# Branch projections over six blocks of 128 rows, the output gate packed to 128 columns, and the branches in the order first, third, second

## The chip, the cores and the metric

The kernel runs on one core of one Trainium2 chip. The metric is the device time of one launch in microseconds. Five engines work side by side: TensorE (PE, with its weight loads shown as PEld), VectorE (DVE), ScalarE (ACT), GpSimd (POOL) and SyncE (SP, which here only issues transfers).

## The reference

Two transformer-like blocks run one after the other on 256 tokens of width 1024. The change lies in the second block, between its input projection and its output projection:

```python
z = h @ w_in[l]                                   # sections: rnn, q, k, v, g, dec, mq, gate
z_rnn, z_q, z_k, z_v, z_g, z_dec, z_mq, z_gate = jnp.split(z, split_idx, axis=-1)
out_a = rg_lru(causal_dwconv(z_rnn, ...), ...)    # gated linear recurrence over the tokens
o_gla = rms_norm(chunked_gla(...), gla_norm[l].reshape(GLA_HEADS, GLA_DV)).reshape(bsz, slen, -1)
out_b = o_gla * jax.nn.silu(z_g)
out_c = ...                                       # attention over mem, 4 heads of 192
branches = jnp.stack([out_a, out_b, out_c], axis=2)            # each 768 wide
proj = jnp.einsum("bsnc,ncd->bsnd", branches, w_branch[l])     # 768 -> 1024, three times
gates = jax.nn.sigmoid(z_gate).reshape(bsz, slen, N_BRANCHES, D_MODEL)
merged = jnp.sum(gates * proj, axis=2)
x = x + merged @ w_out[l]
```

## The kernel before

Every dense product runs weight-stationary over the transposed activations: a weight tile of 128 output columns is [128 rows, 8 blocks, 128 columns] in float32. Each tile is split into a high and a low part in a reduced format (`w_hi`, `w_lo`), each activation likewise, and three products are added: high weights by high and low activations, low weights by high activations. So a tile costs PE 3 x 8 matmuls with 256 moving columns (L629 for the first 16, L634 for the last 8).

The weights pass through a chain of four engines. SP loads a tile into `raw` (L491; two chunks of two tiles each in flight), ACT rounds it into `w_hi` (`round_tile`, L1188, or L1183 and L1185 for a packed tile), POOL subtracts it from `raw` into `w_lo` (`subtract`, L448, or L443 and L444), and PE multiplies. A chunk is two tiles (v = 0, 1). There is one `w_hi` and one `w_lo` for each v: ACT may overwrite `w_hi[v]` when PE has finished its 16 high products, POOL may overwrite `w_lo[v]` when PE has finished the tile, and SP may reload `raw` when POOL has subtracted. The order on each engine is written out by hand: `look_ahead(n)` makes ACT round all tiles up to chunk n at that place of its program; the sections stand in the order of `plan_chunks`.

Widths of 768 are kept as eight blocks of 96 rows (`C96`, `K96 = 8`), so `out_a`, `out_b` and `out_c` fill 96 of 128 partitions and a branch tile is [96 rows, 8 blocks, 128 columns]. Sections in `PACKED` (the recurrence's input `z_rnn`, `zqk`, `zmq`, `mem_k`) spread their eight 96-column tiles over six tiles of 128 columns: the last two tiles are loaded apart into `spare` (L500) and appended as 32 columns each; `evacuate_packed` puts the 32 spilled rows back by two more copies (L1216). The output gate `zg` is not packed: it has eight tiles of 96 columns in four chunks.

What touches the change, in program order of the second block: `z_rnn`, `dec` (a 16-column product, L683), `zqk`, `zv`, `zmq` with the recurrence's gates between, `gate0` beside the memory attention, `zg` beside the linear attention's states (`gla_states`), then `gla_out` (L1061, L1069) and `branch0` in turn, `gate1`, `branch1`, `gate2`, `branch2`, `out2`. On DVE stand in this order: `recur` (the scan, L2163), `silu(0)` and `silu(1)` (L2181), `gla_states(0)` and `(1)` (L2189, L2195), the low part of `out_a` (`rest_parts`, L1739), `silu(2)`, `gla_states(2)` (L2195), `silu(3)`; then the four merges of `branch0` (L2215), the norm of `out_b` (L2233, L2238), its product with the gate (L2242), the low parts of `out_b` and `out_c` (L1739), and the merges (L2217, L2221) with the low parts of `merged` (L2226). ACT rounds the high parts of `out_a`, `out_b` and `out_c` (`round_parts`, L1168) and of `merged` (L1618), and evacuates the gates from PSUM (L1205). PE waits for `outb_split` before `branch1`, for `m_rounded` inside the first product of `out2` (L650).

## Time and profile before

| | us |
|---|---|
| median of 3 runs | 1716.06 (1712.99 to 1716.21) |
| the profiled execution | 1715.97 |
| its span in the trace | 1714.0 |
| PE busy | 1663.0 (97%) |
| DVE / ACT / POOL busy | 1035.4 / 895.0 / 905.3 |

The span is what lies between the first and the last instruction of the trace; 2 us of the run lie outside it. "Busy" of PE is a share of time with a matmul in flight. The stage that the change touches goes from about 1176 to 1468 us of the span.

### The profile page before, as it was taken

How to read it: one execution, taken by the hardware profiler on the slowest of the kernel's cores; microseconds unless marked ns; L12 is line 12 of the kernel's file. 1: busy time of each engine (PE TensorE's matmuls, PEld its weight loads, DVE VectorE, ACT ScalarE, POOL GpSimd, SP SyncE). 2: the span in 40 equal slices, each digit the busy share in tenths (PEclk: the TensorE clock that was granted, in tenths of full speed). 3: DMA queues.
4: the chain of work that ended last, by engine and by line, in shares of the span. 5: the costliest groups of instructions: out<-in, count | busy, mean ns of one | idle time of the engine just before them, and what ended most of it. 6: DMA issues, size and time to landing. Idle time of an engine off the chain costs nothing.

```text
span 1714.0 us, 33864 instructions
## 1 busy us (share of the span) xinstructions
PE 1663.0 (97%) x12837; PEld 1556.6 (91%) x12837; DVE 1035.4 (60%) x1801; ACT 895.0 (52%) x1218; POOL 905.3 (53%) x411
## 2 busy tenths in 40 slices
PE   8998899999999999999999999999999999899997
PEld 7997899899999999998888888898989999799997
DVE  5996755239921777778888666657455263534321
ACT  4555765455555444444444445465676544466652
POOL 7785358668887000000000344467855688588885
PEclk9999999999999999999999999999999999999999
DMA  5564235455556555545555666654533445455663
GB/s 180 169 187 138 75 120 172 146 168 183 183 183 183 169 164 171 161 157 173 174 176 174 209 190 190 192 187 129 161 108 102 124 141 155 135 172 184 183 185 111
DMA packets 80696, 277.02 MB, mean 162 GB/s; under 512 B 10320, under 2 KB 12640, under 8 KB 80608
## 3 DMA queue, kind: packets, MB, share of 16 engines
q1 hardware_dynamic: 80336, 274.76, 51.5%
q8 instruction: 59, 0.97, 0.2%
q0 software_dynamic: 272, 1.05, 0.2%
q14 instruction: 29, 0.24, 0.0%
HBM read 274.73 MB, written 1.05 MB: 161 GB/s over the span
## 4 chain that ended last, share of the span: by engine, by line
PE 88%; DVE 5%; POOL 3%; issue 2%; ACT 1%; DMA 0%; SPq 0%; DVEq 0%; POOLq 0%; ACTq 0%
PE gemm L629 35%; PE gemm L878 20%; PE gemm L634 17%; PE aux L1126 4%; PE gemm L697 3%; PE aux L854 2%; POOL w_lo L448 2%; POOL w_lo L443 1%; PE gemm L661 1%; PE aux L715 1%; DVE big L1724 0%; PE gemm L650 0%; POOL w_lo L444 0%; DVE big L1838 0%; PE aux L823 0%
## 5 line engine op out<-in xcount | busy, mean ns | idle before, releaser
L448 POOL TENSOR_TENSOR w_lo<-raw,w_hi 128x1024 fp32r<-128x1024 f32 (+2 forms) x340 | 825.7, 2435 | 378.8 <-ACT w_hi L1188 367.4
L1188 ACT ACTIVATE w_hi<-raw 128x1024 fp32r<-128x1024 f32 (+2 forms) x500 | 526.5, 1056 | 633.0 <-PE gemm L629 322.5
L629 PE MATMUL gemm<-h_hi,w_hi 128*128 128x256 f32 (+1 forms) x2256 | 325.5, 287 | 1.5 <-PE aux L823 0.7
L629 PE MATMUL gemm<-h_lo,w_hi 128*128 128x256 f32 (+1 forms) x2304 | 324.5, 284 | 0.4 <-DVE mem_lo L1739 0.4
L634 PE MATMUL gemm<-h_hi,w_lo 128*128 128x256 f32 (+1 forms) x2256 | 317.6, 283 | 3.4 <-POOL w_lo L444 2.4
L629 PEld LDWEIGHTS gemm<-h_lo,w_hi 128*128 128x128 f32 (+1 forms) x2304 | 297.9, 192 | 1.0 <-DVE mem_lo L1739 0.9
L629 PEld LDWEIGHTS gemm<-h_hi,w_hi 128*128 128x128 f32 (+1 forms) x2256 | 292.9, 192 | 4.7 <-issue 2.9
L634 PEld LDWEIGHTS gemm<-h_hi,w_lo 128*128 128x128 f32 (+1 forms) x2256 | 290.5, 191 | 5.0 <-POOL w_lo L444 2.8
L448 DVE TENSOR_TENSOR w_lo<-raw,w_hi 128x1024 fp32r<-128x1024 f32 x160 | 195.3, 1222 | 115.5 <-ACT w_hi L1188 113.0
L878 PE MATMUL gemm<-w_hi,h_hi 128*128 128x512 f32 x1024 | 256.7, 393 | 0.0
L878 PEld LDWEIGHTS gemm<-w_hi,h_hi 128*128 128x128 f32 x1024 | 189.8, 188 | 38.1
L580 POOL DMA_DIRECT2D small<-in_memT x1 | 1.0, 1029 | 397.6 <-DVE big L1999 397.6
L878 PE MATMUL gemm<-w_lo,h_hi 128*128 128x512 f32 x512 | 136.9, 389 | 0.0
L2005 DVE TENSOR_TENSOR h_hi<-big,h_hi 128x512 fp32r<-128x512 f32 x64 | 89.3, 1395 | 51.2 <-ACT h_hi L1378 51.2
L878 PEld LDWEIGHTS gemm<-w_lo,h_hi 128*128 128x128 f32 x512 | 96.1, 188 | 20.2
L1769 DVE SCALAR_TENSOR_TENSOR aux<-big,params,aux 128x256 f32<-128x256 f32 x240 | 94.4, 481 | 0.0
L2270 DVE SCALAR_TENSOR_TENSOR big<-gemm,params,big 128x255 f32<-128x255 f32 (+1 forms) x96 | 39.7, 476 | 80.8 <-ACT big L1633 80.8
L443 POOL TENSOR_TENSOR w_lo<-raw,w_hi 128x768 fp32r<-128x768 f32 x24 | 47.1, 1962 | 17.1 <-ACT w_hi L1185 16.9
L1991 DVE TENSOR_TENSOR small<-small 128x512 f16<-128x512 f16 x128 | 50.5, 436 | 0.0
L1988 DVE TENSOR_TENSOR small<-small 128x1024 f16<-128x1024 f16 x64 | 43.8, 685 | 0.0
L1999 DVE SCALAR_TENSOR_TENSOR big<-aux,big 128x512 f32 x64 | 43.8, 684 | 0.0
L854 PEld LDWEIGHTS aux<-small 128*128 128x128 f16 x1024 | 34.5, 97 | 9.7 <-issue 8.1
(359 smaller groups left out, 2010.8 us busy)
## 6 DMA issues: line engine op xcount, KB each, us to landing
raw<-in_w_u SPq DMA_DIRECT2D x128, 512.0 KB, 3.5
raw<-in_w_ev SPq DMA_DIRECT2D x128, 512.0 KB, 3.7
raw<-in_w_up SPq DMA_DIRECT2D x48, 512.0 KB, 4.3
raw<-in_w_gate SPq DMA_DIRECT2D x24, 512.0 KB, 3.6
raw<-in_w_down SPq DMA_DIRECT2D x24, 512.0 KB, 4.3
raw<-in_w_branch SPq DMA_DIRECT2D x24, 384.0 KB, 3.3
raw<-in_w_conv_in SPq DMA_DIRECT2D x16, 512.0 KB, 4.1
raw<-in_w_peer_q SPq DMA_DIRECT2D x16, 512.0 KB, 4.2
```

What stands on the lines that cost most here:

```text
L443: eng.tensor_tensor(lo[:, :, 0:C96], by_k(raw[c.raw][v], C96), hi[:, :, 0:C96], ALU.subtract)
L448: eng.tensor_tensor(w_lo[v][0:rows, 0:n], raw[c.raw][v][0:rows, 0:n], w_hi[v][0:rows, 0:n], ALU.subtract).then_inc(lo_ready[v], 1)
L629: mm = pe.matmul(out, w[:, k, :], act_part[:, k, :], start=(n == k == 0), stop=False)
L634: mm = pe.matmul(out, w[:, k, :], x[0][:, k, :], start=False, stop=(k == KD - 1))
L697: mm = pe.matmul(pair(gemm[c.bank])[:, tt, :], x[:, v * KD // 2 + k, tt * P:(tt + 1) * P], w[:, k, :], start=(begins and tt == k == 0), st ...
L854: mm = pe.matmul(aux[b][:, n * P // 2:(n + 1) * P // 2], hot2[:, b, n // 2, :, n % 2], hot1[:, b, part, n // 2, :, n % 2], start=(part == ...
L878: mm = pe.matmul(gemm[2 * half + tt][:, :], a[:, c.raw, v, tt * P:(tt + 1) * P], w[v][:, half * (D // 2):(half + 1) * (D // 2)], start=Fal ...
L1126: mm = pe.matmul(pair(aux[pr])[:, v, :], w[v][:, k * P:(k + 1) * P], x[:, g * KD + k, :], start=(g == v == k == 0 and w is w_hi and x is f ...
L1188: act.activation(w_hi[v][0:rows, 0:n], raw[c.raw][v][0:rows, 0:n], ACT.Copy).then_inc(hi_ready[v], 1)
L1769: ins = dve.scalar_tensor_tensor(acc, zc[:, k, w:w + T], tap, acc, ALU.mult, ALU.add)
L1991: ins = dve.tensor_tensor(hot1[:, b, part], hot, along(gate_parts[:, part, tokens], P // 2), ALU.mult)
L2005: dve.tensor_tensor(a_lo[:, c.raw, :, :], act_peer[:, plane, :], a_hi[:, c.raw, :, :], ALU.subtract).then_inc(a_split, 1)
```

## The change

It has four parts.

1. **Branch products.** `out_a`, `out_b` and `out_c` get 128 partitions. The last two of their eight blocks of 96 rows are folded into partitions 96 to 127 of the first six, so each is [128 rows, 6 blocks]. A branch weight tile becomes [128 rows, 6 blocks, 128 columns], loaded in three transfers (96 rows of 3 KB, and twice 32 rows of three pieces of 512 bytes). PE does 3 x 6 matmuls for a tile where it did 3 x 8. For `out_a` ACT does the fold by three copies, for `out_c` it is in the last copy from PSUM (three for one), for `out_b` DVE's norm does it (12 instructions for 8).
2. **Output gate.** `zg` is packed: three chunks of 128-column tiles for four of 96. ACT and POOL handle a tile in two instructions; `sg` holds [128, 6, 256] and matches the folded `out_b`. POOL's mask of the scores goes ahead of the third chunk, and DVE does `gla_states(2)` ahead of `silu(2)`.
3. **Order.** The sections run `gate2`, `branch2`, `gate1`, `branch1`; the parts of `out_c` are made before the norm of `out_b`, and the last merges are those of `branch1`.
4. **One rounding moved.** ACT rounds the two tiles of `zqk`'s first chunk before it evacuates the third chunk of `z_rnn`.

```diff
-    for name, count in (("zqk", 3), ("zv", 3), ("zmq", 3), ("gate0", 4), ("zg", 4), ("branch0", 4),
-                        ("gate1", 4), ("branch1", 4), ("gate2", 4), ("branch2", 4), ("out2", 4)):
-        section(name, count)
+    for name, count in (("zqk", 3), ("zv", 3), ("zmq", 3), ("gate0", 4), ("zg", 3), ("branch0", 4),
+                        ("gate2", 4), ("branch2", 4), ("gate1", 4), ("branch1", 4), ("out2", 4)):
+        section(name, count, transfers=3 if name.startswith("branch") else 1)
...
-        a_parts = (x_hi[0:C96], f_hi[0:C96, third[0], :])
+        KB = MW // P
+        a_parts = (x_hi[:, 0:KB, :], f_hi[:, third[0], :][:, 0:KB, :])
...
-        PACKED = ("mem_k", "z_rnn", "zqk", "zmq")
+        PACKED = ("mem_k", "z_rnn", "zqk", "zmq", "zg")
...
+        def fold(tile, j):
+
+            return tile[C96:P, j:KB:KB // 2, :], slice(j * FOLD, (j + 1) * FOLD)
...
+                if c.index in folded:
+                    tile = raw[c.raw][v]
+                    sp.dma_start(tile[0:C96, 0:KB * P], src[:, 0:KB * P]).then_inc(landed[c.raw][v], 16)
+                    for b in range(2):
+                        half = KB // 2 * P
+                        dst = tile[C96:P, b * half:(b + 1) * half].rearrange("r (j m) -> r j m", m=P)
+                        src_b = src[:, (KB + b) * P:(KB + b + 1) * P].rearrange("(j r) m -> r j m", r=FOLD)
+                        sp.dma_start(dst, src_b).then_inc(landed[c.raw][v], 16)
+                    return
...
-                for k in range(KD):
-                    mm = pe.matmul(out, w[:, k, :], x[0][:, k, :], start=False, stop=(k == KD - 1))
+                w = by_k(w_lo[v], m, n=steps)
+                for k in range(steps):
+                    mm = pe.matmul(out, w[:, k, :], x[0][:, k, :], start=False, stop=(k == steps - 1))
...
             for i, c in enumerate(plan["z_rnn"]):
+                look_ahead(plan["zqk"][0].index if i == 2 else c.index + 1)
                 evacuate_packed(c, zr[:, 2 * i:2 * i + 2, RNN_CONV - 1:], zr[:, 6:8, RNN_CONV - 1:])
...
                     act.wait_ge(rnn_done, 1)
-                    round_parts(a_parts[0], out_a, outa_rounded)
+                    for j in range(KB // 2):
+                        dst, rows = fold(all_a, j)
+                        act.activation(dst, out_a[rows, KB:K96, :], ACT.Copy).then_inc(a_folded, 1)
+                    act.wait_ge(a_folded, KB // 2)
+                    round_parts(a_parts[0], all_a, outa_rounded, tiles=KB)
...
-            for i in range(4):
-                if i == 3:
-                    act.wait_ge(out_b_done, 1)
-                    round_parts(b_parts[0], out_b, outb_rounded)
-                gate_evac(1, i)
             act.wait_ge(mo_moved, MH)
-            round_parts(c_parts[0], out_c, outc_rounded)
-            look_ahead(plan["gate2"][0].index)
+            round_parts(c_parts[0], all_c, outc_rounded, tiles=KB)
             for i in range(4):
                 gate_evac(2, i)
-
             for i in range(4):
-                look_ahead(plan["branch2"][i].index + 1)
+                if i == 1:
+                    act.wait_ge(out_b_done, 1)
+                    round_parts(b_parts[0], all_b, outb_rounded, tiles=KB)
+                gate_evac(1, i)
...
-            rest_parts(a_parts[1], out_a, a_parts[0], outa_rounded, outa_split)
+            rest_parts(a_parts[1], all_a, a_parts[0], outa_rounded, outa_split, tiles=KB)
+            gla_states(2)
             silu(2)
-            gla_states(2)
-            silu(3)
```

How the instructions of ACT stand between `z_rnn` and `dec` (L1213 and L1216 take a chunk out of PSUM, L1183 and L1185 round a packed tile, L1205 takes out `dec`). Before, from the evacuation of the second chunk of `z_rnn` on:

```order
L1213 ACTIVATE big<-gemm 96x2x256
L1216 ACTIVATE big<-gemm 32x256 x2
L1213 ACTIVATE big<-gemm 96x2x256
L1216 ACTIVATE big<-gemm 32x256 x2
L1183 ACTIVATE w_hi<-raw 128x8x96
L1185 ACTIVATE w_hi<-big 128x8x32
L1183 ACTIVATE w_hi<-raw 128x8x96
L1185 ACTIVATE w_hi<-big 128x8x32
L1205 ACTIVATE big<-gemm 16x256
```

Of the same place in the changed kernel (its line numbers are 20 higher):

```order
L1233 ACTIVATE big<-gemm 96x2x256
L1236 ACTIVATE big<-gemm 32x256 x2
L1203 ACTIVATE w_hi<-raw 128x8x96
L1205 ACTIVATE w_hi<-big 128x8x32
L1203 ACTIVATE w_hi<-raw 128x8x96
L1205 ACTIVATE w_hi<-big 128x8x32
L1233 ACTIVATE big<-gemm 96x2x256
L1236 ACTIVATE big<-gemm 32x256 x2
L1225 ACTIVATE big<-gemm 16x256
```

The four roundings moved ahead of the second evacuation. On DVE, from the scan to the merges of `branch0`, before:

```order
L2181 TENSOR_TENSOR big<-big,gemm 96x512 x2
L2189 COPY big<-aux 96x2x192 x2
L2195 SCALAR_TENSOR_TENSOR big<-big,aux 96x192 x4
L1739 TENSOR_TENSOR f_hi<-big,x_hi 96x1024 x2
L2181 TENSOR_TENSOR big<-big,gemm 96x512
L2195 SCALAR_TENSOR_TENSOR big<-big,aux 96x192 x4
L2181 TENSOR_TENSOR big<-big,gemm 96x512
L2215 TENSOR_TENSOR big<-big,gemm 128x512 x4
```

and in the changed kernel:

```order
L2211 TENSOR_TENSOR big<-big,gemm 128x512 x2
L2219 COPY big<-aux 96x2x192 x2
L2225 SCALAR_TENSOR_TENSOR big<-big,aux 96x192 x4
L1769 TENSOR_TENSOR f_hi<-big,x_hi 128x768 x2
L2225 SCALAR_TENSOR_TENSOR big<-big,aux 96x192 x4
L2211 TENSOR_TENSOR big<-big,gemm 128x512
L2244 TENSOR_TENSOR big<-big,gemm 128x512 x4
```

One of the gate products is gone and the last states stand ahead of the one that is left. On DVE again, from the merges of `branch0` to the first later merge, before:

```order
L2215 TENSOR_TENSOR big<-big,gemm 128x512 x4
L2233 RECIPROCAL big<-big 96x1024
L2238 SCALAR_TENSOR_TENSOR big<-big,params 96x256 x8
L2242 TENSOR_TENSOR big<-big 96x2048
L1739 TENSOR_TENSOR f_hi<-big,x_lo 96x1024 x2
L1739 TENSOR_TENSOR f_lo<-big,f_hi 96x1024 x2
L2217 TENSOR_TENSOR big<-big,gemm 128x512
```

and in the changed kernel:

```order
L2244 TENSOR_TENSOR big<-big,gemm 128x512 x4
L1769 TENSOR_TENSOR f_lo<-big,f_hi 128x768 x2
L2263 RECIPROCAL big<-big 96x1024
L2268 SCALAR_TENSOR_TENSOR big<-big,params 96x256 x6
L2274 SCALAR_TENSOR_TENSOR big<-big,params 32x256 x6
L2278 TENSOR_TENSOR big<-big 128x1536
L2246 TENSOR_TENSOR big<-big,gemm 128x512
```

The low parts of `out_c` (`f_lo`) moved ahead of the norm; those of `out_b` (`f_hi` from `x_lo`) moved behind the four merges of `branch2`.

## Rows read from the trace of the kernel before

**Rows 1.** The page: the span, and the chain that ended last by engine.

```profile
span 1714.0 us, 33864 instructions
PE 88%; DVE 5%; POOL 3%; issue 2%; ACT 1%; DMA 0%; SPq 0%; DVEq 0%; POOLq 0%; ACTq 0%
```

**Rows 2.** Windows: width, busy PE, PEld, DVE, ACT, POOL (x), granted clock, DMA, GB/s.

```profile
1193.00:1198.00 5.00, 2.98 (x22) 2.39 (x20) 5.00 (x9) 1.25 (x4) 5.00 (x3) 1.00 0.25 84
1198.00:1202.00 4.00, 4.00 (x23) 4.00 (x23) 4.00 (x3) 0.80 (x2) 4.00 (x3) 0.58 0.51 139
1385.00:1398.00 13.00, 9.71 (x75) 9.10 (x76) 9.67 (x6) 8.53 (x10) 10.79 (x4) 1.00 0.23 63
1464.00:1468.00 4.00, 4.00 (x23) 4.00 (x24) 0.49 (x1) 2.33 (x3) 0.40 (x1) 0.61 0.10 39
```

**Rows 3.** The chain in time order, one gate tile: start, length, engine, count.

```profile
1412.08 1.91 PE gemm L629 x16
1413.99 0.96 PE gemm L634 x8
```

**Rows 4.** Timeline, end of `gate1`, start of `branch1`: start, length, instruction, [idle before <-releaser].

```profile
1362.45 6.54 DVE L2233 RECIPROCAL big<-big 96x1024 f32<-96x1024 f32 x1
...
1369.03 10.71 DVE L2238 SCALAR_TENSOR_TENSOR big<-big,params 96x256 f32<-96x256 f32 x8
...
1379.77 4.38 DVE L2242 TENSOR_TENSOR big<-big 96x2048 f32<-96x2048 f32 x1
...
1385.27 2.35 DVE L1739 TENSOR_TENSOR f_hi<-big,x_lo 96x1024 fp32r<-96x1024 f32 x2 [1.13 <-ACT x_lo L1168]
...
1387.68 1.21 PE L629 MATMUL gemm<-x_lo,w_hi 96*128 96x256 f32 x8 [2.85 <-DVE f_hi L1739]
```

**Rows 5.** Timeline around the first tile of `zqk`.

```profile
1185.31 3.68 SPq L491 DMA_DIRECT2D raw<-in_w_zq  x3
...
1191.34 0.85 ACT L1183 ACTIVATE w_hi<-raw 128x768 fp32r<-128x768 f32 x1
...
1194.39 3.15 POOL L444 TENSOR_TENSOR w_lo<-big,w_hi 128x256 fp32r<-128x256 f32 x1
...
1197.59 1.27 PE L634 MATMUL gemm<-h_hi,w_lo 128*128 128x256 f32 x8 [2.02 <-POOL w_lo L444]
```

**Rows 6.** Timeline from the recurrence's scan to the first instruction of `gla_out`.

```profile
1309.57 7.94 DVE L2163 TENSOR_TENSOR_SCAN big<-big 96x256 f32<-96x256 f32 x8
...
1321.04 5.01 DVE L1739 TENSOR_TENSOR f_hi<-big,x_hi 96x1024 fp32r<-96x1024 f32 x2
...
1326.57 1.38 DVE L2195 SCALAR_TENSOR_TENSOR big<-big,aux 96x192 f32<-96x192 f32 x4
...
1328.09 1.57 PE L1061 MATMUL aux<-small,big 64*96 64x64 f32 x32
```

**Rows 7.** Groups by shape, 1130 to 1320 us: count, busy, mean ns, idle before.

```profile
L448 POOL TENSOR_TENSOR w_lo<-raw,w_hi 128x768 fp32r<-128x768 f32 x6 | 11.5, 1929 | 11.0 <-ACT w_hi L1188 10.4 <-PE gemm L634 0.6
...
L1216 ACT ACTIVATE big<-gemm 32x256 f32<-32x256 f32 x24 | 9.1, 378 | 0.3
L1185 ACT ACTIVATE w_hi<-big 128x256 fp32r<-128x256 f32 x22 | 8.8, 402 | 0.0
```

**Rows 8.** DMA issues of the whole run: count, KB each, median us to landing.

```profile
raw<-in_w_branch SPq DMA_DIRECT2D x24, 384.0 KB, 3.3
...
big<-in_rg_w_a SPq DMA_DIRECT2D x1, 288.0 KB, 3.2
...
big<-in_gla_w_decay SPq DMA_DIRECT2D x1, 24.0 KB, 3.9
```

**Rows 9.** Timeline, end of `branch2` and start of `out2`.

```profile
1445.66 15.57 POOL L448 TENSOR_TENSOR w_lo<-raw,w_hi 96x1024 fp32r<-96x1024 f32 x6 [2.25 <-ACT w_hi L1188]
...
1454.18 7.60 DVE L2226 TENSOR_TENSOR m_lo<-big,x_hi 128x512 fp32r<-128x512 f32 x1
...
1463.82 0.51 PE L650 MATMUL gemm<-x_hi,w_hi 128*128 128x256 f32 x2 [2.75 <-ACT x_hi L1618]
```

More of the change, by code:

```diff
@@ L463, in spare_columns @@
             return spare[:, n // 3, :, n % 3 * SPILL:(n % 3 + 1) * SPILL]
-        floats = {c.index: NARROW.get(name, TILE) for name, chunks in plan.items() for c in chunks}
-        tile_rows = {c.index: C96 for name in ("branch0", "branch1", "branch2") for c in plan[name]}
+        floats = {c.index: TILE for c in order}
+        FOLD = P - C96
+        folded = {c.index for name in ("branch0", "branch1", "branch2") for c in plan[name]}
+        floats.update({n: KB * P for n in folded})
+        def fold(tile, j):
+            return tile[C96:P, j:KB:KB // 2, :], slice(j * FOLD, (j + 1) * FOLD)
         ITS = P // (2 * BANKS)
@@ L1090, in _ @@
                     pe.wait_ge(outa_split, 2)
-                    product(plan["branch0"][h0 + i], P, x=a_parts, rows=C96)
+                    product(plan["branch0"][h0 + i], P, x=a_parts, steps=KB)
+            for c in plan["gate2"]:
+                product(c, P)
+            pe.wait_ge(outc_split, 2)
+            for c in plan["branch2"]:
+                product(c, P, x=c_parts, steps=KB)
             for c in plan["gate1"]:
```

119 lines of the change are left out of this document (66 added, 53 removed).

## The prediction

> **What bounds the kernel now.** I read the chain that ended last first: 88% of it is PE [rows 1]. So a matmul taken out of a stretch where PE never waits is worth its own length, and where PE waits, the wait ends when the engine ahead of it ends. The chain in order of time gives the length: 16 matmuls in 1.91 us and 8 in 0.96 us, 0.12 us each, 2.87 us a tile [rows 3]. Then I looked for the places in the touched stage where PE does less than one matmul in 0.12 us. There are four. (1) At 1193 to 1198 us it does 22, and the low products of the first tile of `zqk` wait 2.02 us for POOL [rows 2, 5]; in the 4 us after that the granted clock is 0.58, so PE spends most of them at the lower of its two levels (1.2 for 2.4 GHz), and 23 matmuls are done where 33 would fit [rows 2]. (2) Around 1328 us PE hardly waits, but DVE's chain from the scan ends at 1327.95 and PE's `gla_out` starts at 1328.09 [rows 6]: PE and DVE arrive together, so work taken from PE alone ahead of that point gains nothing. (3) Between 1385 and 1398 us 75 matmuls are done where 109 would fit [rows 2]; PE waits 2.85 us for the low part of `out_b` [rows 4]. (4) At the start of `out2` PE waits 2.75 us for the last part of `merged` [rows 9], and the 4 us after it have a granted clock of 0.61 [rows 2].
>
> **The branch products.** There are 3 sections of 4 chunks of 2 tiles, 24 tiles, and each loses 6 of 24 matmuls: 144 x 0.12 = 17.3 us. A tile then takes PE 18 x 0.12 = 2.15 us. It counts in full only if the three engines behind the weights keep up.
> POOL subtracts [128, 768] in 1929 ns on average [rows 7], under 2.15, where it took 2.60 us a tile in the last branch section (six in 15.57 us [rows 9]). The bounds of what POOL costs are nothing and 24 x (2.60 - 2.15) = 10.8 us; the near row is the one of the same width, so I take 1.0 us, for the last section, where ACT waits for DVE's merge before it rounds on.
> ACT's rounding shrinks with the width (0.85 us for 768 columns [rows 5]) and is well covered.
> The load is the new risk: three transfers for one, on SP's one queue. A buffer's cycle is landing, rounding 0.85, subtraction 1.93 and some 0.4 of handing over, 3.2 us plus the landing, in which PE does four tiles: it binds above 4 x 2.15 - 3.2 = 5.4 us of landing. The whole tile lands in 3.3 us now. The nearest row for short pieces is the load of the recurrence's gate weights, 768 pieces of 384 bytes in 3.2 us, and the third transfer issued right behind it and its twin landed in 3.9 us [rows 8]. With two more issues ahead (under 0.4 us each in the queue) I get 3.9 + 0.7 = 4.6 us: not binding, cost nothing. If it binds, the price is a rival's.
> The Trainium skill speaks against this edit: "DMA: Bandwidth & Descriptors", section Bandwidth, advises large transfers and calls those under 64 KB dominated by their descriptors; two of the three are 48 KB. By the fit in its section on the anatomy of a DMA (about 2.0 us and bytes over 436e3), three in a row would take an estimated 2.7 + 2.1 + 2.1 = 6.9 us, a tile (6.9 + 3.2) / 4 = 2.5 us, and the time would be about 1699 us. The trace's three loads in a row overlap, which speaks for the sum above.
> The fold itself: for `out_c` three copies for one on ACT (378 ns for 256 columns [rows 7], some 0.6 for 512), beside PE's next tiles, nothing. For `out_b` see the order.
>
> **The output gate.** Eight tiles become six: 48 matmuls, 5.8 us of PE. But place (2) says that DVE's chain sets the end. It starts when ACT has rounded the second chunk of `zg` and made the root, now one instruction of 402 ns [rows 7] longer: the scan ends at about 1317.9. ACT then folds `out_a` in three copies (1.8 us) and rounds it in two of 768 columns (1.7): 1321.4, which is when DVE comes free of its states (1321.04 and the 0.4 later [rows 6]). So the fold hides behind DVE, just. The low part of `out_a` took 5.01 us against POOL and 2.35 without it for 1024 columns a piece [rows 4, 6]; three quarters of these are 3.8 and 1.8, for the folded width. The states take 1.38. `gla_out` starts between 1324.6 and 1326.6 in place of 1328.09: a gain of 1.5 to 3.5 us, **2.4**. PE's own work ends before that even with the wait for the first states that shorter cover opens. The bounds are 3.5, and below nothing, -1, if ACT's longer row of copies comes after DVE. What is late next is DVE still.
>
> **The order.** Now `out_b` is ready 21.7 us after the last merge of `branch0`: 6.54 + 10.71 + 4.38 [rows 4]; `gate1` covers 23 us, so its rounding and low part stick out. Afterwards DVE first makes the low parts of `out_c` (2 to 4 us), then 6.54, then twelve instructions at 1.34 = 16.1, then three quarters of 4.38 = 3.3: some 30 us. `branch1` comes 23.0 + 17.2 + 23.0 = 63 us after. The wait goes: 34 missing matmuls, **4.0 us**. `branch2` needs `out_c`, done 5 us into the 23 of `gate2`. DVE's long row now ends 30 us after, when the first merge of `branch2` could go at 27.3; behind it wait four merges, and their PSUM banks are wanted again only at 40, so that costs nothing; without this cover it would be 3 us. On ACT the wait for `out_b` stands behind the first evacuation of `gate1`, at 43 us: over by then. The two roundings of `out_c` put ACT back 1.7 us in a stretch where it has more than that to spare.
>
> **The rounding moved.** ACT rounds the first tile of `zqk` at 1191.34, behind the evacuation of `z_rnn`; its load was issued at 1185.31 [rows 5], so it should be there by 1189 or so. POOL then starts up to 2.4 us earlier, and the 2.02 us wait goes. If the load lands only at 1191, nothing is gained. The pause goes with it, and I expect the clock to stay: 10 matmuls more in the 4 us, 1.2 us. Together **3.2 us**, bounds 0 and 3.5. The evacuations move back by up to 3 us; the convolution on DVE waits for them, but it ends long before its next reader.
>
> **The tail** (4) I leave as it is. DVE's `m_lo` took 7.60 us while POOL ran six subtractions without a pause [rows 9]; a free pair took 2.35 for twice the width each [rows 4]. The Trainium skill ("SBUF — State Buffer", SBUF: two separate sides) has VectorE with two SBUF inputs and GpSimd take one port pair for a whole instruction each, and the trace agrees. What shorter subtractions change here is a rival.
>
> **The sum** against the profiled execution, 1715.97 us (its span 1714.0; the median is 1716.06, so the two agree): -17.3 + 1.0 - 2.4 - 4.0 - 3.2 = -25.9, so **1690 us**.
>
> **Rivals.** *The tail frees itself*: POOL's shorter instructions let `m_lo` in, the last merge is on time, PE's 2.75 us and the 1.2 us at the low clock go: 1686. For it: a gap of 0.2 us in each 2.15. Against: POOL is as busy as before, relative to PE. *POOL binds*: with DVE against it a subtraction keeps 2.6 us, 10.8 for 1.0: 1700. For it: rows 9. Against: rows 7. *The loads line up* so that each waits for the one ahead: 3.3 + 3.9 + 3.9 = 11.1 us of landing, (11.1 + 3.2) / 4 = 3.6 us a tile against 2.87 before, 24 x 0.73 = +17.5, with the other gains of 9.6: 1724, **slower**. It decides from a landing of 8.3 us (branches gain nothing) and 9.9 (the whole is slower). Against: the three loads in a row of rows 8. *The short loads wait for the long one* and overlap each other only: 3.3 + 3.9 = 7.2 us of landing, (7.2 + 3.2) / 4 = 2.6 us a tile, 24 x 0.45 = 10.8 of the 17.3 given back: 1701. This is where the page's rule on small transfers would lead, by its own figures to 1699. *It does not do what it says*: `zg` and the rounding bring nothing (DVE's chain and the load set those ends): 1690 + 2.4 + 3.2 = 1696.
>
> **Chances.** The forecast 0.60, the tail 0.10, POOL 0.11, no gain outside the branches 0.10, short loads behind the long one 0.05, the loads in a row 0.04. The range 1683 to 1700 takes in the first four but for their edges, 0.85 in all. A difference of 0.2% (3.4 us) is about what a measurement of this kernel can tell from none: faster 0.95, same 0.01, slower 0.04.
>
> **What would show it.** A branch tile of 18 matmuls in 2.15 us with no wait of PE for POOL or ACT longer than 0.5 us; landing of the branch loads under 5.4 us; no wait at `branch1`, none of 2 us at `zqk`, the clock 1.0 after it; `gla_out` 2 us earlier relative to the scan. It is wrong if PE waits inside the branch sections, or if ACT comes late with `out_a`.

## The result, and the profile after

| | median of the runs shown | lowest to highest | profiled execution | its span |
|---|---|---|---|---|
| before | 1714.53 us (4) | 1712.80 to 1716.21 | 1715.97 us | 1714.0 us |
| after | 1683.37 us (4) | 1683.01 to 1686.05 | 1683.40 us | 1681.7 us |

The ratio is 0.9822 (95% interval 0.9805 to 0.9839): 1.8% faster, well over the 0.2% that a measurement can tell. The prediction said 1690 us, 25.9 us under the profiled execution of before; the profiled executions are 32.6 us apart. So the direction and the range hold, and 6.7 us more went than the sum has terms for. The rest of this document finds them.

Page of the kernel after: the span, and the chain that ended last, by engine.

```profile
span 1681.7 us, 33548 instructions
PE 90%; DVE 5%; POOL 2%; issue 2%; ACT 1%; DMA 0%; SPq 0%; DVEq 0%; ACTq 0%; POOLq 0%
```

PE is still the bound, and more of it than before [rows 1]. The windows that answer to [rows 2], with the same columns: the first two at `zqk`, the last two at the start of `out2`.

```profile
1191.00:1196.00 5.00, 5.00 (x41) 4.73 (x40) 5.00 (x6) 2.79 (x6) 4.20 (x3) 1.00 0.68 203
1196.00:1200.00 4.00, 4.00 (x35) 4.00 (x35) 4.00 (x4) 3.09 (x6) 3.85 (x4) 1.00 0.44 139
...
1428.00:1432.00 4.00, 2.68 (x20) 2.50 (x21) 3.94 (x3) 1.94 (x3) 4.00 (x2) 1.00 0.73 193
1432.00:1436.00 4.00, 3.90 (x30) 3.49 (x29) 1.71 (x2) 2.12 (x4) 1.07 (x2) 1.00 0.69 209
```

PE does one matmul in some 0.12 us at `zqk`, and the granted clock is 1.00 in all four, where before it was 0.58 and 0.61 after the two waits. To find where the time went I take the start of the same instruction in both traces and follow how the distance between them grows:

| place (start of) | before | after | distance | grown by | forecast |
|---|---|---|---|---|---|
| product of `dec`, ahead of the touched stage | 1189.83 | 1187.72 | 2.11 | 2.11 | 0 |
| decay's matmuls, behind `zqk` | 1214.62 | 1208.74 | 5.88 | 3.77 | 3.2 |
| first `gla_out` | 1328.09 | 1318.54 | 9.55 | 3.67 | 2.4 |
| first product of `out2` | 1458.35 | 1428.54 | 29.81 | 20.26 | 17.3 + 4.0 - 1.0 = 20.3 |
| second chunk of `out2` | 1469.00 | 1436.00 | 33.00 | 3.19 | 0 |
| a product of `up` | 1501.28 | 1469.04 | 32.24 | -0.76 | 0 |

The branches and their order came out as the sum has them. Four things need an explanation: 2.1 us ahead of every touched line, the size of the `zqk` and `zg` terms, and the 3.2 us at `out2`, which the forecast left as it was and one rival gave away.

### The profile page after: what moved, and what is told of

Same layout as the page of the kernel before. It is cut to its first block, busy times and chain, and to the rows that moved or that the text cites. A ratio compares the mean times of both kernels' runs of the same rounds, so it can differ in the third digit from the quotient of the medians.

```text
span 1681.7 us, 33548 instructions
## 1 busy us (share of the span) xinstructions
PE 1638.4 (97%) x12645; PEld 1532.3 (91%) x12645; DVE 1043.7 (62%) x1804; ACT 892.5 (53%) x1226; POOL 894.2 (53%) x415
## 4 chain that ended last, share of the span: by engine, by line
PE 90%; DVE 5%; POOL 2%; issue 2%; ACT 1%; DMA 0%; SPq 0%; DVEq 0%; ACTq 0%; POOLq 0%
PE gemm L649 35%; PE gemm L898 21%; PE gemm L654 18%; PE aux L1146 4%; PE gemm L717 3%; PE aux L874 2%; POOL w_lo L451 1%; PE gemm L681 1%; PE aux L735 1%; DVE big L1754 0%; PE aux L843 0%; PE gemm L703 0%; PE gemm L670 0%; DVE big L1868 0%; DVE big L2193 0%
## 5 line engine op out<-in xcount | busy, mean ns | idle before, releaser
L451 POOL TENSOR_TENSOR w_lo<-raw,w_hi 128x1024 fp32r<-128x1024 f32 (+1 forms) x332 | 800.6, 2420 | 350.9 <-ACT w_hi L1208 339.2
L1208 ACT ACTIVATE w_hi<-raw 128x1024 fp32r<-128x1024 f32 (+1 forms) x492 | 515.6, 1050 | 619.4 <-PE gemm L649 308.0
L649 PE MATMUL gemm<-h_hi,w_hi 128*128 128x256 f32 x2240 | 322.8, 287 | 1.6 <-PE aux L843 0.7
L649 PE MATMUL gemm<-h_lo,w_hi 128*128 128x256 f32 x2288 | 322.6, 284 | 0.4 <-DVE mem_lo L1769 0.4
L654 PE MATMUL gemm<-h_hi,w_lo 128*128 128x256 f32 x2240 | 315.5, 283 | 1.4 <-POOL w_lo L451 0.9
L649 PEld LDWEIGHTS gemm<-h_lo,w_hi 128*128 128x128 f32 x2288 | 296.4, 193 | 1.0 <-DVE mem_lo L1769 0.9
L649 PEld LDWEIGHTS gemm<-h_hi,w_hi 128*128 128x128 f32 x2240 | 290.6, 192 | 4.8 <-issue 3.0
L654 PEld LDWEIGHTS gemm<-h_hi,w_lo 128*128 128x128 f32 x2240 | 288.9, 192 | 3.1 <-POOL w_lo L451 1.8
L447 POOL TENSOR_TENSOR w_lo<-raw,w_hi 128x768 fp32r<-128x768 f32 x30 | 58.8, 1961 | 19.9 <-ACT w_hi L1205 18.5
```

The costliest lines, as they stand in the source:

```text
L447: eng.tensor_tensor(lo[:, :, 0:C96], by_k(raw[c.raw][v], C96), hi[:, :, 0:C96], ALU.subtract)
L451: eng.tensor_tensor(w_lo[v][:, 0:n], raw[c.raw][v][:, 0:n], w_hi[v][:, 0:n], ALU.subtract).then_inc(lo_ready[v], 1)
L649: mm = pe.matmul(out, w[:, k, :], act_part[:, k, :], start=(n == k == 0), stop=False)
L654: mm = pe.matmul(out, w[:, k, :], x[0][:, k, :], start=False, stop=(k == steps - 1))
L1208: act.activation(w_hi[v][:, 0:n], raw[c.raw][v][:, 0:n], ACT.Copy).then_inc(hi_ready[v], 1)
```

## The 2.1 us that the change did not make

The distance is there at 170 us already, in the attention of the first half, on the same instructions (2.40 us; 0.39 of it at 154 us). DVE splits a row of 16 x 256 numbers into parts there while POOL subtracts. The third cast in the trace of before, and in that of after:

```profile
163.21 4.73 POOL L448 TENSOR_TENSOR w_lo<-raw,w_hi 128x1024 fp32r<-128x1024 f32 x2 [1.60 <-ACT w_hi L1188]
...
163.23 2.51 DVE L1798 CAST big<-big 16x256 bf16<-16x256 f32 x1
```

```profile
162.86 0.28 DVE L1828 CAST big<-big 16x256 bf16<-16x256 f32 x1
...
163.16 4.71 POOL L451 TENSOR_TENSOR w_lo<-raw,w_hi 128x1024 fp32r<-128x1024 f32 x2 [1.91 <-ACT w_hi L1208]
...
163.18 2.44 DVE L1831 COPY big<-big 16x256 bf16<-16x256 bf16 x1
```

POOL's two subtractions started at 163.21 in the trace of before and at 163.16 in that of after. The same cast takes 0.28 us when it starts just ahead of POOL's subtraction and 2.5 us when it starts just behind it, since it then waits for the whole of it; so does the copy behind it in either case. A few tenths of a microsecond decide over some 2. The Trainium skill ("SBUF — State Buffer", SBUF: two separate sides) has the pair of ports that VectorE and GpSimd share taken for a whole instruction by whoever starts first; the trace agrees. Whether chance did this, and not the change, I tested with the changed kernel itself.

### The changed kernel again

> The changed kernel itself again, as the yardstick for the two runs beside it. 1683.3 us where the small copies of the attention stage fall the short way and 1685.5 to 1686 where they fall the long way; the runs should show both.

1684.86 us median (1683.50 to 1685.94, 5 runs), beside 1716.11 of before. Its profiled execution took 1685.94 us. Timeline of it:

```profile
163.69 2.50 DVE L1828 CAST big<-big 16x256 bf16<-16x256 f32 x1
...
168.72 1.38 PE L776 MATMUL aux<-big 128*128 128x128 f32 x4 [3.50 <-DVE big L1831]
```

The same program, the other outcome, 2.5 us more, and PE waits 3.5 us for these copies in place of 1.1. So before was profiled with the long outcome and after with the short one. The outcome is the larger part of what differs ahead of the touched stage, but not all of it: from 154 us to 170 it makes 2.0 us between the two traces of the changed kernel, another 0.8 is there ahead of it, and what moves that was not looked for. To set only the long executions side by side is therefore not enough, since `changed_again` came to the product of `dec` 0.98 us later than before did. What holds is the distance from that product on. The table has it for the traces of the experiments that follow, each against the kernel that it was made from: where the product starts, and how much later than in that kernel (minus: earlier) the trace is further on, with the distance at the product taken off.

| trace | against | outcome | product of `dec` | decay's matmuls | first `gla_out` | first of `out2` | second chunk of `out2` |
|---|---|---|---|---|---|---|---|
| `changed_again` | after (1187.72) | long | 1190.81 | 0.0 | 0.0 | 0.0 | 0.0 |
| `round_back` | after | short | 1188.35 | 2.3 | 2.3 | 2.6 | 2.5 |
| `silu_back` | after | short | 1188.04 | 0.0 | 2.3 | 6.7 | 6.6 |
| `old_order` | after | long | 1188.03 | 0.0 | 0.0 | 5.4 | 5.3 |
| `rows_96` | after | long | 1189.60 | 0.0 | 0.0 | 0.2 | 0.2 |
| `one_transfer` | after | long | 1188.63 | 0.0 | 0.0 | 0.3 | 0.3 |
| `loads_held` | after | long | 1190.78 | 0.0 | 0.0 | 8.1 | 7.7 |
| `order_only` | before (1189.83) | short | 1187.46 | 0.0 | 0.0 | -4.1 | -5.6 |
| `columns_768` | before | long | 1190.33 | 0.0 | 0.0 | -0.1 | -3.6 |
| `rows_128` | before | long | 1190.34 | 0.0 | 0.0 | 1.9 | -1.5 |

By this measure the change is worth 30.1 us with the trace of after (32.24 less 2.11) and 30.7 with that of `changed_again`, both at the product of `up`; the sum missed 4.2 to 4.8 us of it, not 6.7. The 0.6 between the two is the clock behind the norm: 0.87 from 1457 to 1469 in the one, 1.00 from 1460 to 1472 in the other.

### POOL held back at that place

```diff
+                    if c is plan["ga"][2]:
+                        subtract(pool, c, tiles=(0,))
+                        pool.wait_ge(c_ready, 1)
+                        subtract(pool, c, tiles=(1,))
+                        continue
```

The first attempt had the wait one chunk too early, at `ga[1]`:

> The changed kernel in which POOL, between the two subtractions of the second chunk of ga, waits until DVE has made the parts of the forget gate's sums. Mine: three small DVE instructions took 2.4 us each there since each waited for a whole subtraction; with POOL held back only the first does, the parts are ready 4.3 us earlier, PE's waits of 1.1 and 4.9 us in that stage shrink by about 4, the time is 1683.3 - 4 = 1679, and all runs lie within 1 us, because no instruction starts beside a subtraction by chance. Rival: POOL's later subtraction makes PE wait instead, and the time stays at 1683; or the small instructions are slow by themselves, and nothing changes but the wait.

1687.39 us (1685.17 to 1688.48). All small instructions took 0.22 to 0.41 us, with POOL silent, which settles that they are not slow by themselves; but that chunk's subtraction was wanted earlier, and PE paid for it:

```profile
154.88 0.28 DVE L1833 CAST big<-big 16x256 bf16<-16x256 f32 x1
...
159.64 2.07 PE L659 MATMUL gemm<-h_hi,w_lo 128*128 128x256 f32 x8 [5.55 <-POOL w_lo L451]
```

The second:

> As pool_waits, but one chunk later: there the wait stood in front of a subtraction that PE needed before the forget gate's sums were ready (PE waited 5.6 us for it), while the subtractions that DVE's small instructions ran into are those of the third chunk of ga. POOL now waits between the two tiles of that chunk. Mine: the first small instruction waits 2.4 us for the first subtraction, all later ones take 0.2 to 0.4, the parts are ready 4.3 us earlier, POOL's second subtraction starts at about 161.3 and ends at 163.7, when PE wants it, and the time is 3 to 4 us under the changed kernel's shorter level, 1679.5. The runs lie closer together than the changed kernel's. Rival: DVE's row of 8 multiplications behind it collides with POOL's subtractions instead, and less than 1 us is left of the gain.

1684.42 us (1682.44 to 1685.07) beside 1684.86 of the changed kernel on the same chip: no difference, where 1679.5 was expected. The parts were ready 4 us earlier, but the eight multiplications behind them now met POOL's subtractions. First the row with POOL held back, then that of the kernel after:

```profile
163.16 7.99 DVE L1845 SCALAR_TENSOR_TENSOR big<-big,params,rstd 128x256 f32<-128x256 f32 x8
```

```profile
167.44 3.48 DVE L1840 SCALAR_TENSOR_TENSOR big<-big,params,rstd 128x256 f32<-128x256 f32 x8
```

The rival of that expectation came true: the collision was moved, not removed. As long as POOL has as many subtractions to make in that stretch, someone on DVE waits for them here.

## The experiments on the four parts

### The rounding of zqk's first tile, put back

```diff
             for i, c in enumerate(plan["z_rnn"]):
-                look_ahead(plan["zqk"][0].index if i == 2 else c.index + 1)
                 evacuate_packed(c, zr[:, 2 * i:2 * i + 2, RNN_CONV - 1:], zr[:, 6:8, RNN_CONV - 1:])
```

> The changed kernel with the rounding of zqk's first tile put back behind the evacuations of z_rnn. Mine: the place gained 3.8 us by the two traces (2.0 us of waiting, the rest clock), so 1683.3 + 3.8 = 1687.1 us, PE waits about 2 us for POOL at zqk and the 4 us after that have a granted clock near 0.6. Rival (the place is only earlier because everything ahead of it is): under 1 us, 1684, no wait. A second thing to read here: in the attention stage of the first half DVE's small copies start either just before or just after a subtraction of POOL, which by the two traces is worth 2.2 us; the profile should show either 0.28 or 2.5 us for the second cast, and its time should lie on the 1687 or the 1689 side accordingly.

1687.16 us median (1686.07 to 1689.53). The profiled one took 1686.73 with the short outcome, 3.3 over 1683.40. Timeline of it, and under it the window behind the wait:

```profile
1196.14 1.22 PE L654 MATMUL gemm<-h_hi,w_lo 128*128 128x256 f32 x8 [2.05 <-POOL w_lo L448]
```

```profile
1196.50:1200.50 4.00, 4.00 (x36) 4.00 (x35) 4.00 (x3) 1.99 (x5) 4.00 (x3) 1.00 0.53 123
```

The wait is back, as long as in [rows 5], but the clock after it is 1.00 here and was 0.58 in [rows 2]. By positions the place costs 2.3 us (2.94 behind `zqk`, 0.63 of them there ahead of it). So the edit is worth 2.3 us, its wait, and 1.5 more in an execution where the clock also falls. In the four traces of kernels with the old rounding in the kernel before (it, `order_only`, `columns_768`, `rows_128`) the stretch from the product of `dec` to the decay's matmuls took 24.8 us, in this one 23.3 and in the changed kernel 21.0. So all four had the 1.5; why this execution was spared is not shown.

Of the kernel after, the load and the rounding of that tile:

```profile
1183.22 3.68 SPq L508 DMA_DIRECT2D raw<-in_w_zq  x3
...
1186.39 0.85 ACT L1203 ACTIVATE w_hi<-raw 128x768 fp32r<-128x768 f32 x1 [2.68 <-DMA raw<-in_w_zq]
```

ACT waits for the load and rounds it 3.2 us after its issue; before, 6.0 us [rows 5]. That the tile would be there in time was the open point of this term.

### The output gate: DVE's row ahead of gla_out

Timeline of the kernel after, from the scan to `gla_out`; it answers to [rows 6].

```profile
1305.28 6.47 DVE L2193 TENSOR_TENSOR_SCAN big<-big 96x256 f32<-96x256 f32 x6
...
1315.28 1.82 DVE L1769 TENSOR_TENSOR f_hi<-big,x_hi 128x768 fp32r<-128x768 f32 x2
1317.01 1.38 DVE L2225 SCALAR_TENSOR_TENSOR big<-big,aux 96x192 f32<-96x192 f32 x4
1318.72 0.69 DVE L2211 TENSOR_TENSOR big<-big,gemm 128x512 f32<-128x512 f32 x1 [0.33 <-ACT big L1594]
```

The low part starts 3.5 us after the scan's end, as before, so the fold did hide. It takes 1.82 us where it took 5.01: mostly ahead of POOL this time. And the multiplication of the third gate pair, 0.69, now stands behind the states; before it lay between the low part and them. The prediction's sum goes from the low part straight to the states, so it took that 0.6 us out of the row without saying so, and did not ask what else the exchange of the two lines does. Putting it back:

```diff
-            gla_states(2)
             silu(2)
+            gla_states(2)
```

> The changed kernel with the multiplication of the third gate pair put back ahead of the last states on DVE. Mine: it costs its own 0.6 us in the row that gla_out waits for and nothing else, so gla_out starts 7.4 us after the end of the scan in place of 6.8, and the time is 0.6 us more, 1684.9, which the times alone can't tell from the changed kernel's 1684.3. Rival: it falls into the time that DVE waits for ACT anyway, gla_out at 6.8.

1690.11 us median (1689.41 to 1692.32), profiled 1690.32 with the short outcome: 6.9 us over the changed kernel (0.3 of it there ahead of the touched stage), where 0.6 was expected. Timeline of it, and under it the windows from `gla_out` on:

```profile
1319.03 0.69 DVE L2211 TENSOR_TENSOR big<-big,gemm 128x512 f32<-128x512 f32 x1 [1.61 <-ACT big L1594]
...
1321.16 2.83 PE L1081 MATMUL aux<-small,big 64*96 64x64 f32 x32 [2.80 <-DVE big L2225]
```

```profile
1320.00:1324.00 4.00, 2.84 (x33) 2.75 (x33) 1.01 (x4) 0.80 (x1) 0.88 (x1) 0.55 0.73 197
1324.00:1328.00 4.00, 4.00 (x25) 4.00 (x26) 0.00 (x0) 1.94 (x6) 0.00 (x0) 0.50 0.00 0
1328.00:1332.00 4.00, 4.00 (x26) 4.00 (x26) 0.00 (x0) 1.50 (x3) 0.31 (x1) 0.67 0.00 0
```

The multiplication needs ACT's third sigmoid, and this now ends late, behind the three folds, two roundings and a rounding of weights. DVE waits 1.61 us for it, the states stand behind that wait, PE waits 2.80 in place of 0.49, and its clock then falls to the lower of its two levels for most of 12 us. `gla_out` starts 2.3 us later by it; between there and `out2` another 4.3 is lost, in a stretch in which PE has no further wait over 0.5 us. So the fold on ACT, "hidden, just" in the sum, is hidden only because this line was moved with it. With it in its old place the gain of the packed gate (3.67) would have become a loss, by these two traces.

### The order of the branches

Old order in the changed kernel (the plan, PE's loops, ACT's and DVE's rows around them; the core of it):

```diff
-                        ("gate2", 4), ("branch2", 4), ("gate1", 4), ("branch1", 4), ("out2", 4)):
+                        ("gate1", 4), ("branch1", 4), ("gate2", 4), ("branch2", 4), ("out2", 4)):
...
-            for i in range(4):
-                merge(2, i)
             rest_parts(b_parts[1], all_b, b_parts[0], outb_rounded, outb_split, tiles=KB)
+            rest_parts(c_parts[1], all_c, c_parts[0], outc_rounded, outc_split, tiles=KB)
             for i in range(4):
                 merge(1, i)
+            for i in range(4):
+                merge(2, i)
```

> The changed kernel with the branches in the order first, second, third again and the low part of out_c behind that of out_b. Mine: the wait for out_b comes back, 4 us less what the shorter low part gives, 1683.3 + 3.5 = 1687, with a stretch ahead of branch1 in which PE waits 2 to 3 us for DVE, and a low clock after it. On the tail: theory A (shorter subtractions let m_lo in) keeps m_lo under 3 us each and no wait of 2 us at out2. Theory B (the order does it) brings the wait of 2.75 us at out2 back and the time to about 1690.

1688.80 us median (1688.05 to 1690.92), 3.9 over the 1684.86 of the changed kernel (on another chip, where before takes 1715.91 for 1716.11); profiled 1688.80 with the long outcome, 2.9 over 1685.94. But this execution came to the touched stage 2.8 us earlier than that one; from there on it loses 5.3 us (the table above). Timeline of it, and PE's windows around the wait's end and behind it:

```profile
1373.65 0.97 PE L649 MATMUL gemm<-x_lo,w_hi 128*128 128x256 f32 x6 [3.82 <-DVE f_hi L1770]
```

```profile
1372.00:1376.00 4.00, 2.35 (x15) 2.32 (x16) 2.41 (x3) 4.00 (x7) 2.72 (x2) 0.85 0.01 2
1376.00:1380.00 4.00, 4.00 (x27) 4.00 (x27) 2.87 (x3) 1.47 (x2) 4.00 (x2) 0.72 0.65 177
```

The wait for `out_b` comes back, and the clock behind it falls. In the kernel after there is none; the last row of DVE's long row, and PE's first product of `branch1`:

```profile
1378.28 3.42 DVE L2278 TENSOR_TENSOR big<-big 128x1536 f32<-128x1536 f32 x1
...
1409.76 0.87 PE L649 MATMUL gemm<-x_lo,w_hi 128*128 128x256 f32 x6
```

The row ends at 1381.7. The last merge of `branch0` ran at 1346.48, so it took 35 us where the prediction had 30 (twelve instructions against POOL took 18.0 us and not 16.1, and the low part of `out_c` 5.9 and not 2 to 4), and it is over 28 us before `branch1`.

The new order alone, in the kernel before (the same lines the other way round):

> The kernel before with the new order of the branches alone, subtractions and products as long as before. Mine: the wait for out_b goes, 1716 - 4.0 = 1712 (or 1713 - 4.0 = 1709 where the attention stage falls the short way). On the tail: theory A (shorter subtractions) leaves one m_lo of 5 to 8 us and a wait of PE of 2 to 3 us at out2. Theory B (the order) frees it, and the time is a further 3 us lower, 1709 or 1706.

1710.49 us median (1708.11 to 1711.36) beside 1715.91, ratio 0.9971 (0.9961 to 0.9982): 5.4 us by the medians, 4.0 forecast. By positions 4.1 us are gained up to `out2`, and 1.5 more behind its start. The low part and the wait there are as they were before, but the clock behind the wait is not: 1.00, where [rows 2] has 0.61.

```profile
1447.71 7.58 DVE L2225 TENSOR_TENSOR m_lo<-big,x_hi 128x512 fp32r<-128x512 f32 x1
...
1457.33 0.51 PE L650 MATMUL gemm<-x_hi,w_hi 128*128 128x256 f32 x2 [2.74 <-ACT x_hi L1617]
```

```profile
1457.00:1461.00 4.00, 3.67 (x30) 3.67 (x31) 0.91 (x2) 3.41 (x5) 0.51 (x1) 1.00 0.18 68
```

### The tail

Timeline of the kernel after at the end of `branch1` and the start of `out2`; it answers to [rows 9].

```profile
1418.33 14.22 POOL L451 TENSOR_TENSOR w_lo<-raw,w_hi 128x768 fp32r<-128x768 f32 x6 [2.03 <-ACT w_hi L1208]
...
1425.17 2.34 DVE L2255 TENSOR_TENSOR m_lo<-big,x_hi 128x512 fp32r<-128x512 f32 x1
...
1428.54 0.47 PE L670 MATMUL gemm<-x_hi,w_hi 128*128 128x256 f32 x2 [0.56 <-ACT w_hi L1208]
```

POOL works without a pause here too (six in 14.22 us, the last two on 1024 columns), and yet `m_lo` waits for one of them only, not for three. (The row of six in [rows 9] holds two of the 128 x 1024 tiles of `out2` as well, its last two, from 1456.5 on. They are the ones that went ahead of the waiting `m_lo`, at the end of the last subtraction on 96 x 1024.) `old_order` showed the same (its `m_lo` at most 2.89 us, no wait for `x_hi`) and `order_only` the opposite. So it is not the order, and it is not a pause of POOL. The subtractions changed in two ways, from 1024 columns to 768 and from 96 rows to 128, and each can be changed alone in the kernel before.

```diff
                 rows = tile_rows.get(c.index, P)
+                n = 6 * P if c in plan["branch2"] else n
                 eng.tensor_tensor(w_lo[v][0:rows, 0:n], raw[c.raw][v][0:rows, 0:n], w_hi[v][0:rows, 0:n],
```

> The kernel before with POOL's subtractions of the third branch cut from 1024 to 768 columns (the low part of the weights' last two blocks is left stale, nothing else changes; PE's products take as long as before). A subtraction then takes about 1.9 of the 2.87 us of a tile. Mine, after old_order and order_only showed that the tail frees itself with the short subtractions and not with the order: m_lo takes under 3 us each, the wait of 2.75 us at out2 goes, 1716 - 3.5 = 1712.5. Rival: it was the pace of PE or the fold, m_lo still takes 7.6 us.

One run, 1713.06 us, with the long outcome in the attention: 2.9 under 1715.97, and by positions 3.5 between the start of `out2` and its second chunk. POOL has a pause here (2.24 us ahead of 1451.65), so this run by itself does not rule one out; `rows_128` does. The `m_lo` that took 7.60 us:

```profile
1454.04 2.35 DVE L2227 TENSOR_TENSOR m_lo<-big,x_hi 128x512 fp32r<-128x512 f32 x1
```

```diff
-                rows = tile_rows.get(c.index, P)
+                rows = P
                 eng.tensor_tensor(w_lo[v][0:rows, 0:n], raw[c.raw][v][0:rows, 0:n], w_hi[v][0:rows, 0:n],
```

> The kernel before with POOL's subtractions of the branch tiles on all 128 rows in place of 96 (the last 32 rows hold the tile before, and nobody reads them): same length, another shape. At the tail m_lo was passed by two subtractions, and both of these came right behind the change from 96 to 128 rows. Theory A (it is the share of its time that POOL is busy): nothing changes, m_lo takes 7.6 us, PE waits 2.7 us, 1716. Theory C (it is the change of shape between two subtractions): m_lo takes 2.9 us, the wait goes, 1713.

1713.56 us median (1711.04 to 1715.64) beside 1716.05, ratio 0.9982 (0.9972 to 0.9993). Timeline of it, its window at the start of `branch1`, and under that the same window of the kernel before.

```profile
1456.63 2.89 DVE L2226 TENSOR_TENSOR m_lo<-big,x_hi 128x512 fp32r<-128x512 f32 x1
```

```profile
1386.00:1398.00 12.00, 9.72 (x55) 9.44 (x56) 7.46 (x5) 7.03 (x8) 9.72 (x4) 0.72 0.24 68
```

```profile
1386.00:1398.00 12.00, 9.71 (x75) 9.10 (x76) 8.95 (x6) 7.53 (x9) 10.79 (x4) 1.00 0.25 69
```

The low part gets in and PE's wait for the last merge is gone, with subtractions as long as before and no pause among them (six in 16.45 us). By positions 3.4 us are gained at `out2`. The profiled execution (1715.64) shows little of it, since behind the same wait of 2.85 us at `branch1` its clock fell: 20 matmuls fewer in that window, 1.9 us by positions. Both halves of the edit thus free the tail, each alone, in the one trace that each has. The last run asks for the opposite, the change of shape in the changed kernel:

```diff
+                rows = C96 if c in plan["branch1"] else P
-                eng.tensor_tensor(w_lo[v][:, 0:n], raw[c.raw][v][:, 0:n], w_hi[v][:, 0:n],
+                eng.tensor_tensor(w_lo[v][0:rows, 0:n], raw[c.raw][v][0:rows, 0:n], w_hi[v][0:rows, 0:n],
```

> The changed kernel with POOL's subtractions of the branch1 tiles on rows 0 to 95 only (the low part of the folded rows is left stale; everything else as it is). Theory C, after rows_128 (a waiting m_lo is passed where POOL goes from a subtraction on 96 rows to one on 128, and gets in where both have 128): in the last branch section the change from 96 to 128 rows comes where the out2 tiles begin, the m_lo that waits there is passed by POOL's next two, takes 6 to 7 us, PE waits 2 to 3 us at out2, and the time is 3 us over the changed kernel's 1684.3, 1687. Theory A (the share of POOL's time, which is the same here): every m_lo under 3 us, 1684.3.

1684.96 us (1683.12 to 1685.63): nothing. Timeline:

```profile
1420.47 14.21 POOL L452 TENSOR_TENSOR w_lo<-raw,w_hi 96x768 fp32r<-96x768 f32 x6 [2.03 <-ACT w_hi L1209]
...
1427.30 2.34 DVE L2256 TENSOR_TENSOR m_lo<-big,x_hi 128x512 fp32r<-128x512 f32 x1
```

So a change from 96 to 128 rows is not enough either, and theory C falls. What is shown: behind a subtraction on 96 x 1024 the waiting `m_lo` is passed by the next two (7.60 and 7.58 us in two kernels), behind 128 x 1024, 96 x 768 and 128 x 768 it isn't passed once (2.89, 2.35 and 2.34). Each edit of the shape also shifts when `m_lo` comes within the subtraction that it waits for, and no run holds one still and moves the other. What decides which of the two engines goes first when a subtraction ends, stays open.

### The three transfers

The branch weights laid out folded, so that a tile is one transfer:

```diff
+def _folded(w):
+    tiles, kb, n, fold = w.shape[0], MW // P, K96 - MW // P, P - C96
+    rest = w[:, :, kb * P:].reshape(tiles, C96 // fold, fold, n, P).transpose(0, 2, 3, 1, 4)
+    return np.concatenate([w[:, :, :kb * P], rest.reshape(tiles, fold, kb * P)], axis=1)
...
+                    sp.dma_start(raw[c.raw][v][:, 0:n], src).then_inc(landed[c.raw][v], 16)
```

> The changed kernel with the branch weights laid out in the folded form beforehand, so that a tile comes in one transfer of 384 KB in place of 288 + 48 + 48. Mine: the three transfers cost nothing, since a tile is there 3.0 us after its issue and up to 5.4 are free; time within 1 us of the changed kernel. Rival (the short transfers slow the section or the queue): 2 to 10 us faster. Landing of a branch tile about 2.9 us.

1683.96 us (1682.54 to 1685.28) beside 1684.86: the same. DMA issues of the kernel after (two rows) and of this one:

```profile
raw<-in_w_branch SPq DMA_DIRECT2D x24, 288.0 KB, 3.0
raw<-in_w_branch SPq DMA_DIRECT2D x48, 48.0 KB, 2.8
```

```profile
raw<-in_w_branch SPq DMA_DIRECT2D x24, 384.0 KB, 3.2
```

By positions too, the two are within 0.3 us of each other at `out2`. The 3.0 and 2.8 us are medians of one transfer each, from its own issue, and not of the tile, which is there when the third has landed; the next run shows that time, since ACT waits for it there. By the Trainium skill ("DMA: Bandwidth & Descriptors", Bandwidth) the two of 48 KB are dominated by their descriptors; they may be, but no one waits for them. To see how much room there was, each branch tile's load was held back until PE is through with the tile after the one that had the buffer:

```diff
                 if c.index in folded:
+                    sp.wait_ge(tile_done[1 - v], last.index + 1 + v)
```

> The changed kernel with each branch tile's load held back until PE has finished the tile after the one that had the buffer (about 4.0 us later than POOL has freed it: 1.9 to PE's end with that tile, 2.11 for the next). It asks how much room the three transfers had. From the changed kernel's trace: landing 3.0, handing over 0.1, rounding 0.85, subtraction 1.85 with 0.3 of handing over make 6.1 us from PE's end of tile n+1 to the low part of tile n+4, which PE wants 5.6 us after it (two tiles and 1.4). So every third tile is 0.5 us late, 0.17 us a tile, 24 tiles: 4 us slower than 1684. By the prediction's own formula, (3.0 + 4.0 + 3.2) / 4 = 2.55 us a tile in place of 2.11: 10 us slower. Rival, there is more room than either says: under 1.5 us slower, no wait of PE for POOL or ACT in the branch sections beyond those of the changed kernel.

1693.45 us (1692.33 to 1693.84), profiled 1693.84 with the long outcome, 7.9 over 1685.94 (the two came to the touched stage at the same time). In its `branch2`, from 1373.00 to 1394.43, a tile takes (21.4 / 8) 2.68 us, against (17.4 / 8) 2.17 in the kernel after. ACT now waits for the landing, where in the kernel after it waits for PE:

```profile
1382.14 0.84 ACT L1209 ACTIVATE w_hi<-raw 128x768 fp32r<-128x768 f32 x1 [2.56 <-DMA raw<-in_w_branch]
```

```profile
1375.20 0.85 ACT L1208 ACTIVATE w_hi<-raw 128x768 fp32r<-128x768 f32 x1 [1.26 <-PE gemm L649]
```

The chain in time order shows one tile of `loads_held` from its first issue to its rounding:

```profile
1383.80 0.32 SPq L502
...
1384.16 0.43 SPq L507
...
1384.63 2.74 DMA raw<-in_w_branch
...
1387.40 0.85 ACT w_hi L1209
```

So the tile is complete 3.6 us after its first issue. For the seven tiles of this section that ACT waits for, taken in their order, it is 3.4 to 4.6, half of them by 3.6. The transfers overlap, but the tile is not there in the 3.0 us that the expectations of both runs count with; the 4.6 of the forecast is the upper end. The prediction's other estimate, 6.9 us, adds up three transfers one behind the other. By the Trainium skill ("DMA: Bandwidth & Descriptors", Anatomy of one DMA — SWDGE (gpsimd) path) the fit behind it is for transfers issued by GpSimd, and these are issued by SP; a tile here took about half of that.

The prediction's formula, landing + 3.2 over four tiles, gives 2.55 us a tile and 10 us in all with a landing of 3.0; my finer one of the expectation gave 4. The coarse one was the nearer, and with 3.6 for the landing it gives (3.6 + 4.0 + 3.2) / 4 = 2.70 us, beside the 2.68 of `branch2`. It had the loads bind at 5.4 us, and 3.6 + 4.0 is past that; how near to 5.4 the edge lies was not tried.

## Why the prediction was right, and what it missed

- **Branch products, -17.3, and POOL's 1.0.** A tile of 18 matmuls takes 2.11 us, no wait of PE over 0.4 in these sections. Timeline of the kernel after in `branch2`:

```profile
1376.12 1.84 POOL L451 TENSOR_TENSOR w_lo<-raw,w_hi 128x768 fp32r<-128x768 f32 x1 [0.27 <-ACT w_hi L1208]
...
1376.36 0.87 PE L649 MATMUL gemm<-f_lo,w_hi 128*128 128x256 f32 x6
1377.06 0.87 PE L654 MATMUL gemm<-f_hi,w_lo 128*128 128x256 f32 x6
```

  POOL's 1.84 fits into it. In `branch1`, where DVE's merges and low parts come between, six subtractions take 14.22 us and PE's section from 1409.76 to 1427.98 takes 18.2 us for 8 x 2.11 = 16.9: 1.3 us, the 1.0 of the sum. From the first `gla_out` to the first product of `out2`, `order_only` takes 126.1 us and the kernel after 110.0: 16.1, where the sum has 16.3.
- **Order, -4.0.** Right in the wait and, in the kernel before, in the size: 4.1 us up to `out2` with the order alone, which with the 16.1 of the branches makes the 20.26 of the table. Undone in the changed kernel it is 5.3. The wait itself was 2.9 us in the kernel before and 3.8 in `old_order`. What comes on top differs: in the kernel before the clock was 1.00 there and PE stood still a few times more, for 0.2 to 0.4 us, in the first tiles of `branch1` (two of these waits are for POOL's low parts); in `old_order` it is the clock, 0.85 and 0.72.
- **Rounding, -3.2.** Measured 3.8: 2.3 for the wait (2.0 in the sum) and 1.5 for the clock behind it (1.2 in the sum). That the clock falls behind this wait is not sure: it did in all four traces with the old rounding in the kernel before, and not in the one with the rounding put back in the changed kernel.
- **Output gate, -2.4.** It was 3.67, above the bound of 3.5. The term that was mis-sized is the low part of `out_a`: the sum has it midway between 1.8 and 3.8 us and it took 1.82, which is 1.0 of the 1.3 us missed; the rest is the scan, which ended 0.1 us later in place of 0.4. Which side of POOL's start it would fall on, the prediction couldn't know. What it did not ask is where `silu(2)` goes: its 0.6 us are in the gain, and moving it is the condition for the rest, since in its old place it costs 2.3 us at `gla_out` and 6.6 in all.
- **The tail, 0.** The term that was wrong in kind. "POOL is as busy as before, relative to PE" was true and no reason: the rival of 4.0 us was right in its effect (3.2 in the table, 3.4 to 3.5 in the two runs that free the tail in the kernel before), though not by a gap of POOL's, which isn't there. Of the 0.8 that is lost again behind it, 0.6 is the clock after the norm, which `changed_again` did not lose.
- **The profiled execution as the base.** The sum was made against one execution, 1715.97. It had the long outcome of a chance worth some 2 us. The times may have said so (1712.99 beside 1716.06 and 1716.21; the first has no trace), and I read no more into them than that the median agrees. So 2.1 of the 6.7 us between forecast and profiled execution is luck, and the 1683.40 is not a better result than 1685.94 of the same program.
- None of the rivals on the loads came true, and POOL did not bind. That POOL's mask stands ahead of the third chunk of `zg`, and the folds of `out_b` and `out_c`, were not undone by themselves; no wait of PE in the traces points at them.

## What to carry to other kernels

Price every line that the diff exchanges, also one of 0.7 us: where it stands in the row that another engine waits for, what counts is when its own input is ready after the change, and that may be later by the very work you add beside it. Where two engines take turns at a port, a wait for one instruction of the other is the least that you can count on, and shape or phase can make it three; ask of each such place what it costs both ways and hold the difference as a range. And before you compare two profiled executions, look at an instruction that neither kernel changed, far ahead of the edit: if it isn't at the same time in both, that difference is not yours, and what you compare is the time from there on.
